# A float32 decoder layer on one core: both feed-forward products by seven block products instead of the second alone

## The chip, the cores and the metric

One core of a Trainium2 chip runs the whole layer in one launch. The metric is the time of an execution on the device in microseconds (us), a median over runs; lower is better. The work is spread over TensorE (PE; its weight loads are listed apart as PEld), VectorE (DVE), ScalarE (ACT), GpSimd (POOL, which here issues DMAs in the feed-forward part) and SyncE (SP, which issues most of the other DMAs).

## The reference

One layer over 512 tokens of width 1024, float32. A mixer comes first (w_in, a gated chunk mixer and a state-space scan, w_out), then the feed-forward part, then a gate with an added per-layer embedding and a last RMSNorm. The change is in the feed-forward part:

```
hid = jax.nn.relu(rmsnorm(h, norm_mlp_g[i]) @ w_ff1[i])   # 512x1024 by 1024x4096
h = h + (hid * hid) @ w_ff2[i]                            # 512x4096 by 4096x1024
```

## The kernel before

**Products.** Every large product is made of three matmuls in the type float32r: each operand is split into a rounded part `hi` and a rest `lo`, and `product` adds hi by hi, lo by hi and hi by lo into one bank of PSUM (lines 1487 to 1489). Each matmul loads 128x128 weights and streams 512 columns. ACT makes `hi` by a copy (`split_form`, line 664), DVE makes `lo` by a subtraction (line 1293).

**Units.** The hidden width of 4096 is worked through in four units of 1024 (`UNITS`). In a unit the first product comes as four *forms* of 512x512 weights of w_ff1 (`product_f1`), each 48 matmuls, an ordinary product. The second product, 512 tokens by 1024 hidden by 1024, is cut in 2x2 blocks and done by Winograd's scheme with seven block products (`product_f2`) of 256 tokens by 512 by 512, 24 matmuls each. Its weight sides are the blocks B11, B21, B22 of w_ff2 and the sums T1 to T4 of blocks; its left sides are blocks A11, A12, A22 of the squared hidden values and sums S1 to S4.

**Forms and buffers.** A form lands in a raw buffer, is split into one of three `ring` buffers, and is then used by PE. The split of form n waits until PE is through with form n-3. There are four raw quarters of 512x512 (`quarter0` to `quarter3`) for w_ff2; the forms of w_ff1 have a raw part in the ring (`ring_raw`). T1 to T4 are summed by DMA: POOL issues a transfer that adds one quarter to another in place (`t_add`, line 568, `quarter<-quarter`), or adds a block from HBM (`quarter<-in_w_ff`). Each form is handled in two pieces, p = 0 and 1, of 512 KB.

**What sets the order.** Each engine runs a list written out by hand, in that order, with semaphores between them: `ff_step` counts PE's steps, `form_hi` and `form_lo` the splits, `q_landed` and `t_landed` the transfers. SP issues loads in a written order too, each after the last reader of its quarter. The results of a second product are added to h by DVE (`h_add`, line 1350) before PE may use the bank again; B11 and T1 are kept in PSUM over all units and added at the end (`h_finish`).

Of the kernel before, what the change touches and what calls it, by code (L numbers as in the profile page):

```python
# [5 lines left out]
P = 128  # L6
F32 = mybir.dt.float32
# [11 lines left out]
TILES = (2, 3, 0, 1)  # L19
UNITS = 4  # L20
STEPS = 30
# [4 lines left out]
SUMS = ("T3", "T2", "T1", "T4")  # L26


def build_layer(nc, a, out):
# [26 lines left out]
    with ExitStack() as ctx:  # L56
# [17 lines left out]
        def form(name, tiles, width):  # L74

            hi = sb(name + "_hi", [P, tiles, width], F32R)
            with ExitStack() as first:
                raw = sb(name + "_raw", [P, tiles, width], where=first)
            lo = sb(name + "_lo", [P, tiles, width], F32R)
            return hi, raw, lo  # L80

        quarter = [sb(f"quarter{i}", [P, 4, 512]) for i in range(2)]
        ring = {0: form("ring0", 4, 512)}
        ring[2] = form("ring2", 4, 512)
        ring[1] = form("ring1", 4, 512)
        quarter += [sb(f"quarter{i}", [P, 4, 512]) for i in range(2, 4)]
        a2 = form("a2", 4, 512)
        s_form = {n: form(f"s{n}", 4, 256) for n in (3, 4, 1, 2)}
        a1 = sb("a1", [P, 4, 512])
        tmp = sb("tmp", [P, 4, 512])  # L90
        with ExitStack() as early:
            conv = sb("conv", [P, 2, 512], where=early)
            xs_t = sb("xs_t", [P, 2, 512], where=early)
# [3 lines left out]
        a11_hi = sb("a11_hi", [P, 4, 256], F32R)  # L97
        a11_lo = sb("a11_lo", [P, 4, 256], F32R)
# [17 lines left out]
        b_hi = sb("b_hi", [P, KT, SEQ], F32R)  # L116
        b_lo = sb("b_lo", [P, KT, SEQ], F32R)
# [77 lines left out]
        f1_landed = [[sem(f"f1_landed{i}{p}") for p in range(2)] for i in range(3)]  # L195
        q_landed = [[sem(f"q_landed{i}{p}") for p in range(2)] for i in range(4)]
        ff_step = sem("ff_step")
        form_hi, form_lo = sem("form_hi"), sem("form_lo")
        gate_hi, gate_lo = sem("gate_hi"), sem("gate_lo")
        t_landed = [[sem(f"t_landed{i}{p}") for p in range(2)] for i in range(2)]  # L200
# [72 lines left out]
        plan += [(("xt", 2, j, q), (2 * j + q + 2) % 4) for j in range(NS) for q in range(2)]  # L273
# [25 lines left out]
        def form_end(n):  # L299

            u, j = divmod(n, FORMS)
            return STEPS * u + (4 * j + 4 if j < 4 else 16 + 2 * (j - 4) + 2)

        def f1_use(n):

            return sum(m % 3 == n % 3 and m % FORMS < 4 for m in range(n + 1))

        def product_end(u, name):

            return STEPS * u + 16 + 2 * PRODUCTS.index(name) + 2  # L310

        def form_count(u, name, p):

            return 2 * (FORMS * u + 4 + PRODUCTS.index(name)) + p + 1

        def hid_bank(u, i):

            return (i + (2 if u else 0)) % 4

        def sum_landed(eng, u, name, p):  # L320

            eng.wait_ge(t_landed[QUARTER[name]][p], 16 * (2 * u + (1 if name in ("T3", "T2") else 2)))

        ADDS = ("T3 right", "T3 above", "T2", "T4", "B21", "B22")
        LAST_ADDS = ("B11 above", "B11 right", "T1 right", "T1 left", "C21", "C12")
# [5 lines left out]
        LO_COUNT = {"A11": 1, "S3": 2, "S2": 3, "S1": 4, "A22": 6, "A12": 6, "S4": 7}  # L331
# [5 lines left out]
        def _(sp):  # L337
# [71 lines left out]
            def load_f1(n):  # L409

                u, e = divmod(n, FORMS)
                b, kh = 2 * u + e // 2, e % 2
                if n >= 3:
                    sp.wait_ge(ff_step, form_end(n - 3))
                else:
                    sp.wait_ge(acc_full, 4 * (OUT + 4) if n < 2 else 4 * (PLE + 1))
                for p in range(2):
                    k = 4 * kh + 2 * p
                    sp.dma_start(ring[n % 3][1][:, 2 * p:2 * p + 2, :], w_ff1[:, k:k + 2, 512 * b:512 * b + 512]
                                 ).then_inc(f1_landed[n % 3][p], 16)  # L420

            def load_quarter(u, name):

                i = QUARTER[name]
                if u:
                    last = {0: "T1", 1: "T4", 2: "B21", 3: "B22"}[i]
                    sp.wait_ge(form_lo, form_count(u - 1, last, 1))
                elif i < 2:
                    sp.wait_ge(lo_ready, 4 * (PLE + 1))
                else:  # L430
                    sp.wait_ge(acc_full, 4 * (PLE + 1))
                row, col = int(name[1]) - 1, int(name[2]) - 1
                for p in range(2):
                    k = 8 * u + 4 * row + 2 * p
                    sp.dma_start(quarter[i][:, 2 * p:2 * p + 2, :], w_ff2[:, k:k + 2, 512 * col:512 * col + 512]
                                 ).then_inc(q_landed[i][p], 16)

            def reload_b12(u):

                for p in range(2):  # L440
                    sum_landed(sp, u, "T2", p)
                    sp.wait_ge(form_lo, form_count(u, "T3", p))
# [3 lines left out]

            load_f1(0)
            load_f1(1)
            load_quarter(0, "B12")
            load_quarter(0, "B11")  # L450
            for s in range(NS):
                sp.wait_ge(*emptied(PLE, s))
                sp.dma_start(ple_dram[s], y[:, s, :]).then_inc(ple_stored[s], 16)
            load_f1(2)
            load_quarter(0, "B22")
            load_quarter(0, "B21")
            load_f1(3)
            reload_b12(0)
            for u in range(1, UNITS):
                load_quarter(u, "B12")  # L460
                load_quarter(u, "B11")
                load_quarter(u, "B21")
                load_f1(FORMS * u)
                load_quarter(u, "B22")
                for e in range(1, 4):
                    load_f1(FORMS * u + e)
                reload_b12(u)

            last = UNITS - 1
            sp.wait_ge(s_raw, 7 * UNITS)  # L470
            sp.wait_ge(hid_lo, 7 * last + LO_COUNT["A11"])
            load_gain(a["final_norm_g"], 0)
            for p in range(4):
                sp.wait_ge(form_lo, form_count(last, "T1" if p < 2 else "T4", 1))
                sp.dma_start(w_raw[:, p], w_gate[:, 2 * p:2 * p + 2, 0:512]).then_inc(w_landed[p], 16)
            sp.wait_ge(ff_step, product_end(last, "T1"))
# [15 lines left out]
        def _(pool):  # L492
# [56 lines left out]
            def t_add(u, name, p):  # L549

                at = (slice(None), slice(2 * p, 2 * p + 2))
                k = 8 * u + 2 * p
                if name == "T3":
                    pool.wait_ge(q_landed[0][p], 16 * (2 * u + 1))
                    pool.wait_ge(q_landed[3][p], 16 * (u + 1))
                    src = quarter[3][at]
                elif name == "T2":
                    sum_landed(pool, u, "T3", p)
                    pool.wait_ge(form_lo, form_count(u, "B11", p))
                    src = quarter[0][at]  # L560
                elif name == "T1":
                    pool.wait_ge(q_landed[0][p], 16 * (2 * u + 2))
# [1250 lines left out]
```

## Time and profile before

| | before |
|---|---|
| median of 3 runs | 748.6 us (747.29 to 748.61) |
| the profiled execution | 747.09 us |
| its span in the trace | 745.3 us |
| PE busy | 735.0 us, 99% |
| DVE, ACT, POOL busy | 61%, 51%, 14% |
| TensorE clock granted | 0.997 of full, mean |

The profiled execution's time is 1.8 us more than its span; that difference lies around the trace. Busy time of PE counts a matmul until its modelled end, and these overlap: a matmul that reads 0.39 us long starts 0.23 us after the one before it, so start-to-start distances are the price of one, not the durations.

### The profile page before, as it was taken

To read this page: it belongs to the slowest core of one execution; us is meant where nothing else is said; L and a number is where in the kernel's file an instruction comes from. 1 tells how busy PE (TensorE), PEld (TensorE's weight loads), DVE (VectorE), ACT (ScalarE), POOL (GpSimd) and SP (SyncE) were. 2 spreads that over 40 slices of the span, in tenths; PEclk is the share of its full clock that TensorE was granted. 3 is DMA by queue.
4 is the path that set the end of the run, shared out by engine and by line. 5 is a ranking of instruction groups with operands and counts; after the bars stand their busy time and mean duration, and the time that the engine had idled before them with its cause. 6 is when DMAs were issued, how large, how long until landed. Compare 5 with 4: busy or idle time off the path is not lost.

```text
span 745.3 us, 8676 instructions
## 1 busy us (share of the span) xinstructions
PE 735.0 (99%) x3396; PEld 606.4 (81%) x3396; DVE 454.1 (61%) x500; ACT 382.9 (51%) x516; POOL 107.3 (14%) x88
## 2 busy tenths in 40 slices
PE   8999999999999999999999999999999999999996
PEld 7888877788878888888888888888888888888884
DVE  5556794576667465546444952576454942589764
ACT  6524456644674833304564633572266524575775
POOL 1031000766455000000012000020001000200000
PEclk9999999999999999999999999999999999999998
DMA  9732223342241163100976685477727792585311
GB/s 332 210 86 86 87 85 99 124 143 86 93 162 57 57 214 125 58 29 14 373 234 148 140 297 150 84 143 231 227 63 156 192 275 97 118 192 178 106 57 56
DMA packets 47872, 105.58 MB, mean 142 GB/s; under 512 B 4668, under 2 KB 6360, under 8 KB 47832
## 3 DMA queue, kind: packets, MB, share of 16 engines
q1 hardware_dynamic: 40968, 84.03, 33.7%
q0 software_dynamic: 5632, 16.78, 12.4%
q10 hardware_dynamic: 1232, 4.23, 1.6%
q8 instruction: 27, 0.44, 0.2%
q14 instruction: 13, 0.11, 0.0%
HBM read 88.21 MB, written 4.23 MB: 124 GB/s over the span
## 4 chain that ended last, share of the span: by engine, by line
PE 98%; DMA 1%; ACT 0%; issue 0%; DVE 0%; SPq 0%; DVEq 0%
PE acc L1487 28%; PE acc L1489 28%; PE acc L1488 28%; PE side L1549 3%; PE side L1488 2%; PE side L1489 2%; PE side L1487 2%; PE side L1646 2%; PE side L1613 1%; PE side L1653 1%; PE side L1641 1%; DMA gain<-in_norm_mix_g 1%; PE acc L1570 0%; PE side L1593 0%; PE side L1594 0%; PE side L1633 0%
## 5 line engine op out<-in xcount | busy, mean ns | idle before, releaser
L1487 PE MATMUL acc<-w_hi,a_hi 128*128 128x512 f32 x256 | 104.5, 408 | 0.0
L1489 PE MATMUL acc<-w_hi,a_lo 128*128 128x512 f32 x256 | 100.2, 391 | 0.0
L1488 PE MATMUL acc<-w_lo,a_hi 128*128 128x512 f32 x256 | 99.9, 390 | 0.0
L1487 PE MATMUL acc<-b_hi,ring_hi 128*128 128x512 f32 x256 | 99.7, 390 | 0.0
L1489 PE MATMUL acc<-b_hi,ring_lo 128*128 128x512 f32 x256 | 99.7, 389 | 0.0
L1488 PE MATMUL acc<-b_lo,ring_hi 128*128 128x512 f32 x256 | 99.7, 389 | 0.0
L664 ACT ACTIVATE ring_hi<-quarter 128x1024 fp32r<-128x1024 f32 x56 | 56.5, 1051 | 51.3 <-PE acc L1489 34.7
L1293 DVE TENSOR_TENSOR ring_lo<-ring_raw,ring_hi 128x1024 fp32r<-128x1024 f32 x32 | 38.6, 1223 | 67.0 <-ACT ring_hi L664 67.0
L1293 DVE TENSOR_TENSOR ring_lo<-quarter,ring_hi 128x1024 fp32r<-128x1024 f32 x56 | 66.0, 1220 | 17.0 <-ACT ring_hi L664 17.0
L568 POOL DMA_DIRECT2D quarter<-quarter x24 | 20.8, 868 | 351.1 <-DMA quarter<-in_w_ff 223.1
L993 DVE TENSOR_TENSOR w_lo<-w_raw,w_hi 128x1024 fp32r<-128x1024 f32 (+1 forms) x40 | 50.8, 1272 | 27.9 <-ACT w_hi L587 27.4
L664 ACT ACTIVATE ring_hi<-ring_raw 128x1024 fp32r<-128x1024 f32 x32 | 33.8, 1056 | 59.3 <-DMA ring_raw<-in_w_ff 59.3
L1487 PEld LDWEIGHTS acc<-w_hi,a_hi 128*128 128x128 f32 x256 | 48.2, 188 | 11.1 <-issue 1.4
L1488 PEld LDWEIGHTS acc<-w_lo,a_hi 128*128 128x128 f32 x256 | 48.2, 188 | 10.6 <-issue 1.4
L1489 PEld LDWEIGHTS acc<-w_hi,a_lo 128*128 128x128 f32 x256 | 48.1, 188 | 10.4
L1488 PEld LDWEIGHTS acc<-b_lo,ring_hi 128*128 128x128 f32 x256 | 48.1, 188 | 10.0
L1487 PEld LDWEIGHTS acc<-b_hi,ring_hi 128*128 128x128 f32 x256 | 48.1, 188 | 10.0
L1489 PEld LDWEIGHTS acc<-b_hi,ring_lo 128*128 128x128 f32 x256 | 48.1, 188 | 9.9
L1487 PE MATMUL acc<-w_hi,b_hi 128*128 128x512 f32 x128 | 50.5, 395 | 0.0
L1489 PE MATMUL acc<-w_hi,b_lo 128*128 128x512 f32 x128 | 50.0, 391 | 0.0
L1488 PE MATMUL acc<-w_lo,b_hi 128*128 128x512 f32 x128 | 49.9, 390 | 0.0
L587 ACT ACTIVATE w_hi<-w_raw 128x1024 fp32r<-128x1024 f32 (+1 forms) x40 | 40.2, 1007 | 15.9 <-PE acc L1489 13.7
(231 smaller groups left out, 1471.8 us busy)
## 6 DMA issues: line engine op xcount, KB each, us to landing
quarter<-in_w_ff SPq DMA_DIRECT2D x40, 512.0 KB, 4.8
w_raw<-in_w_in SPq DMA_DIRECT2D x36, 512.0 KB, 3.7
ring_raw<-in_w_ff SPq DMA_DIRECT2D x32, 512.0 KB, 4.9
quarter<-quarter POOLq DMA_DIRECT2D x24, 512.0 KB, 6.1
w_raw<-in_w_out SPq DMA_DIRECT2D x16, 512.0 KB, 3.4
h<-in_x SPq DMA_DIRECT2D x8, 512.0 KB, 4.3
seg<-cs_dram ACTq DMA_DIRECT2D x8, 512.0 KB, 3.9
quarter<-in_w_ff POOLq DMA_DIRECT2D x8, 512.0 KB, 6.3
```

The costliest lines, as they stand in the source:

```text
L568: pool.dma_start(quarter[QUARTER[name]][at], src, accum_op=ALU.add).then_inc(t_landed[QUARTER[name]][p], 16)
L587: act.activation(w_hi[:, half, 2 * p:2 * p + n, :], w_raw[:, p, 0:n, :], ACT.Copy, scale=scale).then_inc(hi_ready, 1)
L664: act.activation(hi[at], src, ACT.Copy).then_inc(form_hi, 1)
L993: ins = dve.tensor_tensor(lo, raw, hi, ALU.subtract)
L1293: dve.tensor_tensor(lo[at], src, hi[at].bitcast(F32), ALU.subtract).then_inc(form_lo, 1)
L1487: pe.matmul(dst, st[0], mv[0], start=start, stop=False)
L1488: pe.matmul(dst, st[0], mv[1], start=False, stop=False)
L1489: return pe.matmul(dst, st[1], mv[0], start=False, stop=stop)
L1549: ins = pe.transpose(bank[:, i * P:i * P + P], src(i), ident[:])
L1613: filled(pe.matmul(bank.rearrange("p (c n) -> p c n", c=NS), wsT[:, g, :], h[:, :, g * P:g * P + P], start=True, stop=True), ("mix", g))
L1641: filled(pe.matmul(bank, bcT[:, 2 + g, at], carry[:], start=True, stop=True), ("off", j))
L1646: ins = pe.matmul(bank[:, r * HD:r * HD + HD], lm[:, r, :], xdt[:, r * HD:r * HD + HD], start=True, stop=True)
```

## The change

The first product is now done by the seven products too. In each unit the weight sides are blocks of w_ff1 and their sums, in the order `FIRST`, and the left sides (x, shared by all units) are A11, A12, S4, S2, S3, S1, A22 of the normed h, made once ahead of the first unit. A block product of the first product has 256 tokens as its moving side and writes four groups of 256 columns in a pair of banks. DVE then combines the seven results into the four blocks of hidden values (`combine`), after ACT copied two of them out of PSUM (`copy_product`). All weights now go through the four quarters, 14 forms in a unit. T4 is summed in the third buffer, from T2; T1 of the first product is made by DVE (`make_t1`). B22 of the second product now comes fifth. SP's loads stand in the order in which the buffers are released.

```diff
-FORMS = 11
-PRODUCTS = ("B11", "T3", "T2", "T1", "T4", "B21", "B22")
-A_FORMS = ("A11", "S3", "S2", "S1", "A22", "A12", "S4")
-QUARTER = {"T3": 0, "T1": 0, "B12": 0, "B11": 1, "T2": 1, "T4": 1, "B21": 2, "B22": 3}
+FORMS = 14
+FIRST = ("B11", "B21", "B22", "T2", "T3", "T1", "T4")
+FIRST_A = ("A11", "A12", "S4", "S2", "S3", "S1", "A22")
+SECOND = ("B11", "B21", "T3", "T2", "B22", "T1", "T4")
+SECOND_A = ("A11", "A12", "S3", "S2", "S4", "S1", "A22")
+QUARTER = {"T3": 0, "B12": 0, "B11": 1, "T2": 1, "B21": 2, "T4": 2, "B22": 3}
...
+            def load_quarter(u, m, name):
...
+                    if m:
+                        last_use = {"B12": "T3", "B11": "T2", "B22": "T1", "B21": "T4"}[name]
+                        sp.wait_ge(form_lo, form_count(u, 0, last_use, p))
...
+            for u in range(UNITS):
+                load_quarter(u, 1, "B12")
+                load_quarter(u, 1, "B11")
+                load_quarter(u, 1, "B22")
+                load_quarter(u, 1, "B21")
+                reload_b12(u)
+                if u < UNITS - 1:
+                    load_quarter(u + 1, 0, "B11")
+                    load_quarter(u + 1, 0, "B22")
+                    load_quarter(u + 1, 0, "B12")
+                    load_quarter(u + 1, 0, "B21")
...
+            def combine(u, what):
+
+                dst, left, right, op = {
+                    "C11": ("A11", "A21", pair(1), ALU.add), "U": ("A21", pair(1), "A21", ALU.subtract),
+                    "C12 part": ("A12", "A12", "A21", ALU.add), "U3": ("A21", "A21", pair(0), ALU.add),
+                    "C12": ("A12", "A12", pair(1), ALU.add), "C22": ("A22", "A21", pair(1), ALU.add),
+                    "C21": ("A21", pair(0), "A21", ALU.subtract)}[what]
...
+            def product_f1(u, j):
...
+                if j < 2:
+                    pe.wait_ge(*((h_added, add_count(u - 1, ("B22", "T4")[j])) if u else emptied(PLE, 2 + j)))
+                elif j in (2, 4):
+                    pe.wait_ge(p_copied, 2 * u + j // 2)
+                else:
+                    pe.wait_ge(combined, combined_count(u, {3: "C11", 5: "U", 6: "U3"}[j]))
...
+                        ins = product(pair(j % 2)[:, i, :], [t[:, k, i * P:i * P + P] for t in (hi, lo)],
+                                      [t[name][:, k, :] for t in (x_hi, x_lo)], k == 0, k == 3)
```

PE's list at the start of the feed-forward part, before:

```order
L1487 MATMUL acc<-b_hi,ring0_hi 128x512
L1488 MATMUL acc<-b_lo,ring0_hi 128x512
L1489 MATMUL acc<-b_hi,ring0_lo 128x512
L1487 MATMUL acc<-b_hi,ring0_hi 128x512
L1488 MATMUL acc<-b_lo,ring0_hi 128x512
```

And of the change at the same place:

```order
L1641 MATMUL acc<-xA11_hi,ring0_hi 128x256
L1642 MATMUL acc<-xA11_lo,ring0_hi 128x256
L1643 MATMUL acc<-xA11_hi,ring0_lo 128x256
L1641 MATMUL acc<-xA11_hi,ring0_hi 128x256
L1642 MATMUL acc<-xA11_lo,ring0_hi 128x256
```

The 192 matmuls of 512 columns of a unit's first product have become 336 of 256 columns; the second product keeps 168 of 512.

DVE's list in the third unit around the second product, before (`s` and `a2` are left sides):

```order
L1332 TENSOR_TENSOR a2_lo<-a2_raw,a2_hi 128x1024 x2
L1293 TENSOR_TENSOR ring2_lo<-quarter0,ring2_hi 128x1024 x2
L1350 TENSOR_TENSOR h<-h,acc 128x2x512 x2
L1332 TENSOR_TENSOR s4_lo<-s4_raw,s4_hi 128x1024
L1293 TENSOR_TENSOR ring0_lo<-quarter1,ring0_hi 128x1024 x2
L1350 TENSOR_TENSOR h<-h,acc 128x2x512
```

And of the change, in the second unit, from the last `combine` (line 1455; `fS4_raw` is also A21's buffer) to the left side S2:

```order
L1455 TENSOR_TENSOR fS4_raw<-acc,fS4_raw 128x1024
L1476 TENSOR_TENSOR fA12_lo<-fA12_raw,fA12_S1_hi 128x1024
L1429 TENSOR_TENSOR ring2_lo<-quarter0,ring2_hi 128x1024 x2
L1469 TENSOR_TENSOR fS3_raw<-fS4_raw,fA11_S4_raw 128x1024
L1469 TENSOR_TENSOR fS1_raw<-fS4_raw,fA22_raw 128x1024
L1476 TENSOR_TENSOR fS3_lo<-fS3_raw,fS3_hi 128x1024
L1429 TENSOR_TENSOR ring0_lo<-quarter1,ring0_hi 128x1024 x2
L1469 TENSOR_TENSOR fS2_raw<-fA11_S4_raw,fS1_raw 128x1024
L1469 TENSOR_TENSOR fS4_raw<-fA12_raw,fS2_raw 128x1024
L1493 TENSOR_TENSOR h<-h,acc 128x2x512
L1476 TENSOR_TENSOR fS2_lo<-fS2_raw,fA11_S2_hi 128x1024
```

The blocks of hidden values are combined, squared by ACT, subtracted and split while PE is in the first three products of the second product; before, all of A's first half was ready ahead of it.

POOL's list of adding transfers, before, two units:

```order
L568 DMA quarter0<-quarter3 128x1024 x2
L568 DMA quarter1<-quarter0 128x1024 x2
L568 DMA quarter0<-in_w_ff2 128x2x512 x2
L568 DMA quarter1<-quarter2 128x1024 x2
L568 DMA quarter0<-quarter3 128x1024 x2
L568 DMA quarter1<-quarter0 128x1024 x2
L568 DMA quarter0<-in_w_ff2 128x2x512 x2
L568 DMA quarter1<-quarter2 128x1024 x2
```

And of the change, one unit:

```order
L647 DMA quarter0<-quarter3 128x1024 x2
L647 DMA quarter1<-quarter0 128x1024 x2
L647 DMA quarter2<-quarter1 128x1024 x2
L647 DMA quarter0<-quarter3 128x1024 x2
L647 DMA quarter1<-quarter0 128x1024 x2
L647 DMA quarter2<-quarter1 128x1024 x2
L647 DMA quarter0<-in_w_ff2 128x2x512 x2
```

Eight adding transfers in a unit have become 14, and each of T3, T2 and T4 is now made from the one before it.

## Rows read from the trace of the kernel before

**Rows 1.** The page: span, busy time, granted clock in 40 slices.

```profile
span 745.3 us, 8676 instructions
PE 735.0 (99%) x3396; PEld 606.4 (81%) x3396; DVE 454.1 (61%) x500; ACT 382.9 (51%) x516; POOL 107.3 (14%) x88
PEclk9999999999999999999999999999999999999998
```

**Rows 2.** The page's chain that ended last, by engine.

```profile
PE 98%; DMA 1%; ACT 0%; issue 0%; DVE 0%; SPq 0%; DVEq 0%
```

**Rows 3.** Windows: the four units and the rest behind them.

```profile
core 0: us, PE busy (x) PEld busy (x) DVE busy (x) ACT busy (x) POOL busy (x), PEclk, DMA share, GB/s
363.80:445.40 81.60, 81.60 (x362) 67.62 (x361) 47.14 (x43) 38.44 (x47) 9.43 (x10) 1.00 0.77 226
527.00:608.60 81.60, 81.60 (x362) 67.61 (x361) 45.90 (x42) 38.36 (x45) 7.96 (x9) 1.00 0.64 169
690.20:745.30 55.10, 47.95 (x224) 39.62 (x222) 34.23 (x57) 36.72 (x68) 0.00 (x0) 0.96 0.19 69
```

**Rows 4.** Timeline of PE, two matmuls 24 apart: start, duration.

```profile
454.19 0.39 PE L1487 MATMUL acc<-b_hi,ring_hi 128*128 128x512 f32 x1
...
459.63 0.39 PE L1487 MATMUL acc<-b_hi,ring_hi 128*128 128x512 f32 x1
```

**Rows 5.** Timeline: a weight load between two matmuls.

```profile
402.28 0.39 PE L1489 MATMUL acc<-b_hi,ring_lo 128*128 128x512 f32 x1
402.28 0.19 PEld L1487 LDWEIGHTS acc<-b_hi,ring_hi 128*128 128x128 f32 x1
402.51 0.39 PE L1487 MATMUL acc<-b_hi,ring_hi 128*128 128x512 f32 x1
```

**Rows 6.** Chain in order of time: float32 matmuls of 512 and of 64 columns.

```profile
132.71 1.72 PE side L1613 x4
...
146.46 1.73 PE side L1646 x16
```

**Rows 7.** Groups by line in 330 to 700 us: splits and additions.

```profile
L1293 DVE TENSOR_TENSOR ring_lo<-quarter,ring_hi 128x1024 fp32r<-128x1024 f32 x56 | 66.0, 1220 | 17.0 <-ACT ring_hi L664 17.0
L1350 DVE TENSOR_TENSOR h<-h,acc 128x1024 f32<-128x1024 f32 x23 | 28.0, 1219 | 24.8 <-PE acc L1489 24.3
L664 ACT ACTIVATE ring_hi<-quarter 128x1024 fp32r<-128x1024 f32 x56 | 56.5, 1051 | 51.3 <-PE acc L1489 34.7 <-PE side L1489 13.7 <-DMA quarter<-quarter 2.8
```

**Rows 8.** Timeline: two splits back to back on DVE, and on ACT.

```profile
495.52 2.35 DVE L1332 TENSOR_TENSOR s_lo<-s_raw,s_hi 128x1024 fp32r<-128x1024 f32 x2
...
572.51 1.99 ACT L664 ACTIVATE ring_hi<-quarter 128x1024 fp32r<-128x1024 f32 x2
```

**Rows 9.** The page's DMA queues: packets, MB, share of 16 engines.

```profile
q1 hardware_dynamic: 40968, 84.03, 33.7%
q0 software_dynamic: 5632, 16.78, 12.4%
```

**Rows 10.** Landing times of SP's loads of quarters (line 435), of POOL's adding transfers (line 568).

```profile
DMA to landing us min/median/max: 3.8/4.9/11.6
...
DMA to landing us min/median/max: 4.5/6.2/9.7
```

**Rows 11.** Waits in 330 to 745 us: total, times, longest.

```profile
DVE ring_lo L1293 <- ACT ring_hi L664: 84.0, 27, 6.7
```

**Rows 12.** DVE in the last unit, and PE's first transposes for the gate.

```profile
680.17 2.55 DVE L1365 TENSOR_TENSOR h<-h 128x1024 f32<-128x1024 f32 x2
...
688.27 0.87 PE side L1549 x8
```

More of the change, by code:

```diff
@@ L72, in build_layer @@
             gain = sb("gain", [P, 2, D], where=early)
[L74 to L91, printed above, removed]
+            tmp = sb("tmp", [P, 4, 512], where=early)
             conv = sb("conv", [P, 2, 512], where=early)
             xs_t = sb("xs_t", [P, 2, 512], where=early)
+        def split_pair(name, tiles, width):
+            return sb(name + "_hi", [P, tiles, width], F32R), sb(name + "_lo", [P, tiles, width], F32R)
@@ new lines, in raw_lo, with raw_hi @@
+        def raw_lo(name):
+            with ExitStack() as first:
+                raw = sb(name + "_raw", [P, 4, 256], where=first)
+            return raw, sb(name + "_lo", [P, 4, 256], F32R)
+        def raw_hi(name):
+            with ExitStack() as first:
+                raw = sb(name + "_raw", [P, 4, 256], where=first)
+            return raw, sb(name + "_hi", [P, 4, 256], F32R)
+        quarter = [sb(f"quarter{i}", [P, 4, 512]) for i in range(2)]
+        ring = {0: split_pair("ring0", 4, 512)}
@@ new lines, in build_layer @@
+        ring[2] = split_pair("ring2", 4, 512)
+        ring[1] = split_pair("ring1", 4, 512)
+        quarter += [sb(f"quarter{i}", [P, 4, 512]) for i in range(2, 4)]
+        with ExitStack() as early:
+            g_hi = sb("g_hi", [P, KT, SEQ], F32R, where=early)
+            g_lo = sb("g_lo", [P, KT, SEQ], F32R, where=early)
+        x_hi, x_lo, x_raw = {}, {}, {}
+        for name in ("A11", "A12"):
+            x_hi[name], x_lo[name] = split_pair("x" + name, 4, 256)
+        x_raw["A11"], x_hi["S2"] = raw_hi("xA11_S2")
@@ L94, in build_layer @@
+        f_raw["S2"], f_lo["S2"] = raw_lo("fS2")
+        f_lo["A12"] = sb("fA12_lo", [P, 4, 256], F32R)
+        f_raw["S3"], f_lo["S3"] = raw_lo("fS3")
+        f_raw["S1"], f_lo["S1"] = raw_lo("fS1")
         with ExitStack() as early:
@@ L297, in freed, with form_of @@
             ins.then_inc(side_free[fills[name][0]], 1)
-        def form_end(n):
+        def form_of(n):
             u, j = divmod(n, FORMS)
[L302 to L325, printed above, removed]
+            return u, j // 7, (FIRST + SECOND)[j]
+        def form_index(u, m, name):
+            return FORMS * u + 7 * m + (FIRST, SECOND)[m].index(name)
@@ L327, in add_count, with pair @@
+        def pair(i):
+            return acc[:, 2 * i:2 * i + 2, :].rearrange("p a (b n) -> p (a b) n", b=2)
+        ADDS = ("B21", "T3 right", "T3 above", "T2", "B22", "T4")
+        LAST_ADDS = ("B11 above", "B11 right", "T1 right", "C12", "T1 left", "C21")
         def add_count(u, what):
             return 2 + len(ADDS) * u + ADDS.index(what) + 1
-        LO_COUNT = {"A11": 1, "S3": 2, "S2": 3, "S1": 4, "A22": 6, "A12": 6, "S4": 7}
+        COMBINED = ("C11", "U", "C12 part", "U3", "C12", "C22", "C21")
@@ L687, in split_a @@
[L687 to L698 removed]
+                i = home(m, name)
@@ new lines, in _ @@
+                both(5)
+                both(6)
+                both(7)
+                both(8)
+                hidden(u, "A12")
+                split_a(u, "A12")
+                hidden(u, "A22")
+                both(9)
+                hidden(u, "A21")
+                split_a(u, "S3")
+                both(10)
+                split_a(u, "S2")
+                split_a(u, "S4")
+                both(11)
+                both(12)
+                split_a(u, "S1")
+                both(13)
```

699 lines of the change are left out of this document (381 added, 318 removed).

## The prediction

> **What bounds the kernel now.** I read the page first: PE is busy for 735.0 of 745.3 us at the full granted clock [rows 1], and the chain that ended last is 98% PE [rows 2]. Only what shortens PE's list or makes it wait can matter. The windows cut the feed-forward part into four units of 81.6 us, PE busy in all of each, with DVE busy for 45.9, ACT for 38.4 and the DMA engines for 0.64 of it [rows 3]. The timeline gives PE's price: 24 matmuls of 512 columns start over 459.63 - 454.19 = 5.44 us, so 226.7 ns each [rows 4]. A unit has 192 + 168 = 360 of them, and 360 x 226.7 ns = 81.6 us: the whole window, so PE waits for nothing in it. Four units are 326.4 us.
>
> **PE's list.** The first product's 768 matmuls of 512 columns (174.1 us) become 1344 of 256 columns, 12.5% fewer columns. The trace has no float32r matmul of 256 columns, so its price is bounded. From below: half of 226.7 is 113.3 ns, if all of the price goes with the columns. There is a floor near that: float32 records of 512 columns cost 1.72 / 4 = 430 ns each, but those of 64 columns 1.73 / 16 = 108 ns, twice what an eighth of 430 would be [rows 6]. Each has its own load of 128x128 weights, so I read 108 ns as the price of a load, and 256 columns stay above it. From above: a load reads 188 ns long and begins as the matmul before it starts [rows 5]; if the next load could only start when the current matmul does, a matmul would cost 226.7 however short. The 108 ns of [rows 6] speak against that, since loads must overlap each other there. Between the ends I take 120 ns: 512 ticks of the 2.4 GHz level are 213.3 ns, 13.4 are left, and I keep them as a fixed part, 106.7 + 13.4. Then 1344 x 0.120 = 161.3 us, 12.8 less than 174.1. At 113.3 ns it is 152.3, 21.8 less. Break-even is 174.1 / 1344 = 129.5 ns.
>
> The Trainium skill (TensorE: Matmul & The Clock Gate, "Back-to-back issue gap") has N / 2.4 + 2.5 ns for an isolated gap. By that 512 columns would cost 216 ns and 256 would cost 109, and the first product would come out at 146.7 us, 27 less. The 226.7 of [rows 4] for 512 is more than that page has, so I don't take its short fixed part.
>
> **DVE and ACT.** Back to back, an operation of 128x1024 costs 2.35 - 1.22 = 1.13 us on DVE and 1.99 - 1.05 = 0.94 us on ACT [rows 7, 8]; additions that read PSUM last the same 1.22 us [rows 7]. DVE's list for a unit is now 28 splits of forms, 7 combines, 2 for T1, 7 splits and 4 differences of left sides and 6 additions to h: 54 operations, 61 us, where a unit will be 336 x 0.120 + 168 x 0.2267 = 78.4 us. ACT has 28 + 2 copies + 8 for ReLU and square + 7 = 45, 42 us. So neither is the bound on average; before they were at 45.9 and 38.4 of 81.6 [rows 3].
>
> They can be late in one place. Let product 5 of a unit (T1, counted from 0) end at 0. A block product lasts 48 x 0.120 = 5.76 us in the first product and 5.44 in the second, so product 6 ends at 5.8, product 9 starts at 16.6 and product 10, which needs S2, at 22.1. ACT's list from 0 on: form 8 (1.9), ReLU, square and split of A12 (4.9), the same without split for A22 (6.9), form 9 (8.8), ReLU and square of A21, whose last part comes after product 6 (10.8). Then DVE's difference S3 (12.1), ACT's split of it (13.1) and of form 10 (15.1), DVE's rest of form 10 (16.3), the differences S2 and S4 (18.8), B21's addition to h (19.9), and the rest of S2 at 21.1. That is 1.0 us ahead of product 10. The start is less sure than that: form 8 is B21 of w_ff2, loaded into the third quarter only after form 6 (T4) was split, and form 6's split waits for product 3, which ended at -11.5, and on DVE for two combines behind it. It is through at -7.7 and -6.6; with 4.9 us to landing [rows 10] the pieces are there at -2.8 and -1.7. But the two adding transfers of T3 stand in the same DMA engines then. By [rows 9] a piece of 0.524 MB holds all 16 engines for 0.337 x 745.3 / 84.03 x 0.524 = 1.6 us as a load and 0.124 x 745.3 / 16.78 x 0.524 = 2.9 us as an addition. Two of these in between make the second piece land at about 3, where ACT wants it at 1. So the chain comes out up to 1 us late for product 10, and 3 us where both additions and a load collide. I take 1.2 us of waiting for each unit, 4.8 in all, between 0 and 12.
>
> In the first unit the x side is added: 4 differences and 5 splits on DVE and their copies on ACT, in front of or between the splits of forms 1 to 5. It starts as soon as the last tile is transposed, with two forms ahead, and costs 9 x 1.13 = 10 us on DVE out of the 17 us of slack (78.4 - 61). I take 1.5 us, between 0 and 5. Behind the last product, the first transposes of the gate [rows 12] need T1's addition and C12's, which before were over 5 us earlier: 680.17 + 2.55 = 682.7 against 688.27. Now both come after product T1, 2 x 1.2 = 2.4 us against half of T4's 5.44, 2.7. I take 0.2, at most 2. Copies out of PSUM and combines sit one product (5.8 us) ahead of the bank's next use with two or three operations before them; at nothing, and 1.1 us for each operation that is late.
>
> **DMA.** A unit has 18 loads and 14 adding transfers: 18 x 1.6 + 14 x 2.9 = 69 us of the DMA engines in 78.4 us, 88%, where before it was 18 x 1.6 + 8 x 2.9 = 52 in 81.6, 0.64, as the window shows [rows 3]. It fits, with little left. The chain T3, T2, T4, each after the other, has two rounds in a unit. A round is a load (4.9), three additions (3 x 6.2, [rows 10]) and a split (2.3): 26 us of half a unit's 39. POOL only issues.
>
> **Sum.** -12.8 + 4.8 + 1.5 + 0.2 = -6.3. Against the profiled execution's 747.1 that is 740.8. The median of the runs shown is 1.5 above it, and I predict that: 742.3 us.
>
> **Rivals.**
> *Cheaper still.* The price goes with the columns (113 ns) and waiting is small: -21.8 + 6 = -16, 733 us. For it: that nothing in the trace says the 13.4 ns are fixed. Against: the shorter PE's part, the earlier it asks for DVE's, so that waits grow where PE's list shrinks.
> *Waiting eats it all, slower.* The place above: if the chain to S2 and the one to S4 behind it (form 11, two additions to h and a split, 5.7 us against a product of 5.44) are late together by over 3.2 us in each unit, the 12.8 are gone. With 5 us for each unit the sum is -12.8 + 20 + 1.7 = +9, 757 us. For it: DVE has 13 operations in a row there with no gap; DVE now waits 84.0 us for ACT's halves over the part [rows 11], and every such wait inside this stretch goes to PE. Against: only the late piece of form 8 starts it.
> *The DMA engines become the bound.* If packets take a quarter longer than now, 69 becomes 86 us for each unit, 4.6 more than 81.6: +18, 765 us. It decides from 18% on. For it: adding transfers already took up to 9.7 us [rows 10]. Against: in the first unit 0.77 was held without a wait [rows 3].
> *Loads don't overlap short matmuls.* A matmul of 256 columns then costs 108 + 107 = 215 ns, 289 us for the 1344, +115, 862 us. Against it: by the same rule 512 columns would cost 108 + 213 = 321, and [rows 4] has 226.7. The Trainium skill (TensorE: Matmul & The Clock Gate, "What overlaps and what doesn't") has loads overlap running matmuls only when the row group differs, which here it never does; the trace disagrees, since in [rows 5] the load runs inside the matmul.
> *No change.* The waits make up 11 to 14 us: within 0.2%.
>
> **Numbers.** The forecast (1.5 to 13 us faster) has 0.58, cheaper still 0.10, no change 0.10, waiting 0.12, DMA 0.07, loads 0.03. About 0.2% (1.5 us) is what a measurement of this kernel can tell from no change. So faster 0.68, the same 0.10, slower 0.22. The range leaves out the loads, the DMA rival and half of the waiting above, and the far end of the cheap case below: 732 to 753 us.
>
> **What the profile after would show.** The first product's matmuls 120 ns apart (right), 113 or over 130 (wrong). DVE busy for about 61 us and ACT for 42 in a unit, DMA share near 0.88. PE idle, if anywhere, ahead of the second product's third to fifth block products, released by DVE's `lo` of S2 or S4, 1 to 1.5 us a unit. T3's and T2's additions landing in under 9 us. It would be wrong if PE waits over 3 us a unit, if transfers of T2 or of the reloaded B12 end ACT's waits in every round, or if the price is over 129 ns.

## The result and the profile after

| | before | after |
|---|---|---|
| median of 4 runs | 747.94 us (747.23 to 748.61) | 754.92 us (752.95 to 756.94) |
| the profiled execution | 747.09 us | 752.95 us |
| its span | 745.3 us | 751.2 us |

The ratio is 1.0094, 95% interval 1.0062 to 1.0125: the change makes the kernel 7 us slower, where 742.3 us (732 to 753) had been forecast. The profiled execution is its fastest, 2.0 us under its median, and shows 5.9 of them.

The page after, in the parts that answer to [rows 1, 2, 9, 10] (span, busy time; queues with their share of 16 engines; the chain that ended last, by engine and by line; landing times):

```profile
span 751.2 us, 10013 instructions
PE 729.8 (97%) x3972; PEld 625.7 (83%) x3972; DVE 529.2 (70%) x553; ACT 415.7 (55%) x525; POOL 128.0 (17%) x112
...
q1 hardware_dynamic: 40968, 84.03, 33.7%
q0 software_dynamic: 9088, 29.36, 21.2%
...
PE 71%; DVE 10%; DMA 9%; ACT 7%; issue 3%; SPq 0%; ACTq 0%; DVEq 0%
PE acc L1641 20%; PE acc L1643 20%; PE acc L1642 20%; DMA quarter<-in_w_ff 8%; DVE ring_lo L1429 4%; PE side L1706 3%; ACT ring_hi L769 2%; PE side L1803 2%; DVE h L1493 1%; ACT fA_raw L781 1%; DVE fS_lo L1476 1%; ACT fA_S_hi L802 1%; PE side L1770 1%; PE side L1641 1%; DVE fS_raw L1469 1%
...
quarter<-in_w_ff SPq DMA_DIRECT2D x72, 512.0 KB, 6.7
quarter<-quarter POOLq DMA_DIRECT2D x48, 512.0 KB, 6.1
```

The chain, 98% PE before, is 71% PE now. DMA, DVE and ACT stand in it with 26%: the path that ends last goes through loads of w_ff blocks and the splits and sums made from them. q0, the queue of the adding transfers, carries 29.36 MB where it carried 16.78. A load of a quarter now lands after 6.7 us in the median, where it took 4.8 to 4.9 before; an addition as before after 6.1.

Windows of the same kernel, cut at the switches between first and second product, then the gate (they answer to [rows 3]):

```profile
core 0: us, PE busy (x) PEld busy (x) DVE busy (x) ACT busy (x) POOL busy (x), PEclk, DMA share, GB/s
365.90:406.20 40.30, 40.30 (x338) 40.30 (x337) 37.10 (x33) 24.60 (x25) 4.77 (x7) 1.00 0.84 214
406.20:450.50 44.30, 40.66 (x171) 32.48 (x170) 36.54 (x32) 27.06 (x27) 7.96 (x9) 0.96 0.94 224
450.50:490.80 40.30, 40.30 (x338) 40.30 (x337) 27.97 (x24) 22.03 (x23) 5.84 (x7) 1.00 0.74 185
490.80:530.20 39.40, 39.01 (x171) 31.30 (x170) 33.62 (x29) 21.76 (x22) 7.08 (x9) 1.00 0.99 240
530.20:570.50 40.30, 40.30 (x338) 40.30 (x337) 29.09 (x25) 23.23 (x24) 5.79 (x7) 1.00 0.73 184
570.50:609.80 39.30, 38.68 (x170) 31.31 (x169) 33.62 (x29) 21.40 (x22) 6.99 (x8) 1.00 0.98 240
609.80:650.10 40.30, 40.30 (x337) 40.27 (x336) 29.09 (x25) 22.18 (x23) 5.57 (x7) 1.00 0.75 184
650.10:692.40 42.30, 39.91 (x179) 32.20 (x178) 39.78 (x38) 25.29 (x30) 4.34 (x5) 1.00 0.80 222
692.40:743.30 50.90, 48.05 (x217) 39.48 (x215) 31.75 (x51) 35.31 (x65) 0.00 (x0) 0.97 0.13 48
```

Read the lengths first. All four first products take 40.3 us, which is 336 x 0.120: not one wait, and 12.8 us less for the four than the 174.1 of the kernel before. The second products should take 168 x 0.2267 = 38.1 us each. They take 44.3, 39.4, 39.3 and 42.3 (0.9 of the last are the gate's first transposes): 6.2 + 1.3 + 1.2 + 3.3 = 12.0 us too long. The gate behind them takes 50.9 us, where before it took 46.2 (691.7 to 737.9): 4.7 more. The feed-forward part begins 1.5 us later, at 365.9 instead of 364.4 (PE's first matmul of w_in starts at 12.6 instead of 10.8, and 0.3 of that is made up on the way), and the end behind the gate is 0.5 longer. In all -12.8 + 12.0 + 4.7 + 1.5 + 0.5 = +5.9, which is the difference of the two spans.

The list of PE's waits after, from 365 us on (total, times, longest):

```profile
PE acc L1641 <- DVE fS_lo L1476: 3.4, 2, 2.6
PE acc L1641 <- DVE w_lo L1107: 2.9, 1, 2.9
PE side L1706 <- DVE h L1506: 1.4, 1, 1.4
PE acc L1641 <- DVE fA_lo L1476: 1.1, 1, 1.1
PE side L1641 <- DVE fS_lo L1476: 0.6, 2, 0.5
```

`fS_lo` and `fA_lo` are left sides of the second product, `w_lo` is the gate's weights, `h` is C12's last addition ahead of the transposes. These are 9.4 us. In the first unit PE waits at product 8 for A12 (1.1) and at product 9 for S3 (2.6); products are counted from 0 in a unit, 7 to 13 being the second product's. The rest of the 16.7 lies in shorter delays and in this (timeline of PE after, around the wait of 2.6 us, then around the one of 2.9):

```profile
418.25 0.39 PE L1643 MATMUL acc<-ring_hi,fA_lo 128*128 128x512 f32 x1
421.20 0.58 PE L1641 MATMUL acc<-ring_hi,fS_hi 128*128 128x512 f32 x1 [2.57 <-DVE fS_lo L1476]
421.58 0.63 PE L1642 MATMUL acc<-ring_lo,fS_hi 128*128 128x512 f32 x1
422.01 0.63 PE L1643 MATMUL acc<-ring_hi,fS_lo 128*128 128x512 f32 x1
...
710.76 0.50 PE L1641 MATMUL acc<-w_hi,g_hi 128*128 128x512 f32 x1 [2.85 <-DVE w_lo L1107]
...
712.39 0.63 PE L1643 MATMUL acc<-w_hi,g_lo 128*128 128x512 f32 x1
712.82 0.63 PE L1641 MATMUL acc<-w_hi,g_hi 128*128 128x512 f32 x1
```

Behind both waits the matmuls start 0.43 us apart instead of 0.227. The windows of those two stretches show it as granted clock:

```profile
711.50:714.90 3.40, 3.40 (x10) 2.63 (x9) 2.52 (x4) 1.65 (x6) 0.00 (x0) 0.52 0.02 5
421.40:424.80 3.40, 3.40 (x9) 2.64 (x9) 3.37 (x4) 0.60 (x2) 2.42 (x2) 0.51 0.48 110
```

So in each of the two windows PE runs at 1.2 instead of 2.4 GHz, which costs about 1.7 of their 3.4 us.

**What is behind the wait of the first unit.** The timelines of SP, POOL, ACT and DVE after, for B21 of w_ff2 (form 8, third quarter):

```profile
387.12 4.06 ACT L769 ACTIVATE ring_hi<-quarter 128x1024 fp32r<-128x1024 f32 x4
390.47 1.22 DVE L1171 TENSOR_TENSOR xA_lo<-xA_raw,xA_hi 128x1024 fp32r<-128x1024 f32 x1
391.61 1.22 DVE L1476 TENSOR_TENSOR fA_lo<-fA_S_raw,fA_S_hi 128x1024 fp32r<-128x1024 f32 x1
392.74 1.22 DVE L1455 TENSOR_TENSOR fS_raw<-acc,fS_raw 128x1024 f32<-128x1024 f32 x1
394.06 1.23 DVE L1455 TENSOR_TENSOR fA_raw<-fA_raw,fS_raw 128x1024 f32<-128x1024 f32 x1
395.21 2.35 DVE L1429 TENSOR_TENSOR ring_lo<-quarter,ring_hi 128x1024 fp32r<-128x1024 f32 x2
396.45 1.50 SPq L517 DMA_DIRECT2D quarter<-in_w_ff  x2
397.25 0.85 POOL L647 DMA_DIRECT2D quarter<-quarter  x1 [19.85 <-DMA quarter<-in_w_ff]
398.52 0.85 POOL L647 DMA_DIRECT2D quarter<-quarter  x1 [0.42 <-issue]
407.37 1.06 ACT L769 ACTIVATE ring_hi<-quarter 128x1024 fp32r<-128x1024 f32 x1 [4.65 <-DMA quarter<-in_w_ff]
```

ACT has made its half of T4 (form 6) by 391.2. Four operations of DVE stand ahead of DVE's half: x's A22, A11's split and the combines U and C12 part. So that half starts at 395.21; the two loads of B21 follow it, and the two additions of T3 are issued between and behind them. The second piece, issued at 397.6, lands 9.8 us later, at 407.4. ACT has been waiting 4.65 us for it. Everything behind on ACT and DVE (A12, A22, S3) is late by that: product 8 waits for A12, and product 9, which needs S3, waits 2.6 us behind 418.25.

### The profile page after: what moved, and what is told of

The parts are those of the page before. It is cut to its first block, busy times and chain, and to the rows that moved or that the text cites. A ratio compares the mean times of both kernels' runs of the same rounds, so it can differ in the third digit from the quotient of the medians.

```text
span 751.2 us, 10013 instructions
## 1 busy us (share of the span) xinstructions
PE 729.8 (97%) x3972; PEld 625.7 (83%) x3972; DVE 529.2 (70%) x553; ACT 415.7 (55%) x525; POOL 128.0 (17%) x112
## 3 DMA queue, kind: packets, MB, share of 16 engines
q1 hardware_dynamic: 40968, 84.03, 33.7%
q0 software_dynamic: 9088, 29.36, 21.2%
## 4 chain that ended last, share of the span: by engine, by line
PE 71%; DVE 10%; DMA 9%; ACT 7%; issue 3%; SPq 0%; ACTq 0%; DVEq 0%
PE acc L1641 20%; PE acc L1643 20%; PE acc L1642 20%; DMA quarter<-in_w_ff 8%; DVE ring_lo L1429 4%; PE side L1706 3%; ACT ring_hi L769 2%; PE side L1803 2%; DVE h L1493 1%; ACT fA_raw L781 1%; DVE fS_lo L1476 1%; ACT fA_S_hi L802 1%; PE side L1770 1%; PE side L1641 1%; DVE fS_raw L1469 1%
## 5 line engine op out<-in xcount | busy, mean ns | idle before, releaser
L769 ACT ACTIVATE ring_hi<-quarter 128x1024 fp32r<-128x1024 f32 x112 | 113.3, 1050 | 94.3 <-PE acc L1643 47.2
L1429 DVE TENSOR_TENSOR ring_lo<-quarter,ring_hi 128x1024 fp32r<-128x1024 f32 x112 | 132.8, 1221 | 41.4 <-ACT ring_hi L769 41.3
L647 POOL DMA_DIRECT2D quarter<-quarter x48 | 41.4, 862 | 341.8 <-DMA quarter<-in_w_ff 249.8
L1642 PE MATMUL acc<-xS_lo,ring_hi 128*128 128x256 f32 x256 | 72.4, 283 | 0.0
L1100 DVE TENSOR_TENSOR w_lo<-w_raw,w_hi 128x1024 fp32r<-128x1024 f32 x36 | 48.1, 1337 | 27.7 <-ACT w_hi L668 27.3
L1641 PEld LDWEIGHTS acc<-w_hi,a_hi 128*128 128x128 f32 x256 | 48.1, 188 | 10.8 <-issue 1.4
L1643 PEld LDWEIGHTS acc<-w_hi,a_lo 128*128 128x128 f32 x256 | 48.0, 188 | 10.4
L1643 PE MATMUL acc<-xA_hi,ring_lo 128*128 128x256 f32 x192 | 54.3, 283 | 0.0
L1641 PE MATMUL acc<-xS_hi,ring_hi 128*128 128x256 f32 x192 | 54.3, 283 | 0.0
L1643 PE MATMUL acc<-xS_hi,ring_lo 128*128 128x256 f32 x192 | 54.3, 283 | 0.0
L1642 PE MATMUL acc<-xA_lo,ring_hi 128*128 128x256 f32 x192 | 54.3, 283 | 0.0
L1641 PE MATMUL acc<-xA_hi,ring_hi 128*128 128x256 f32 x192 | 54.3, 283 | 0.0
L1642 PEld LDWEIGHTS acc<-xS_lo,ring_hi 128*128 128x128 f32 x256 | 49.2, 192 | 0.0
L1641 PE MATMUL acc<-a_hi,w_hi 128*128 128x512 f32 x96 | 38.9, 405 | 0.0
L1643 PE MATMUL acc<-ring_hi,fS_lo 128*128 128x512 f32 x96 | 38.1, 396 | 0.0
```

Of the source, the lines that this page charges most:

```text
L647: pool.dma_start(quarter[home(m, name)][at], src, accum_op=ALU.add).then_inc(t_landed[home(m, name)][p], 16)
L769: act.activation(ring[n % 3][0][at], quarter[i][at], ACT.Copy).then_inc(form_hi, 1)
L1100: ins = dve.tensor_tensor(lo, raw, hi, ALU.subtract)
L1429: dve.tensor_tensor(lo[at], src, hi[at].bitcast(F32), ALU.subtract).then_inc(form_lo, 1)
L1641: pe.matmul(dst, st[0], mv[0], start=start, stop=False)
L1642: pe.matmul(dst, st[0], mv[1], start=False, stop=False)
```

## The experiments

Ratios are to the kernel before, with the 95% interval.

**The change again, unaltered, and three edits of one order each.**

> The changed kernel unaltered, to compare the others with on one chip. Theory 1 (waits at few fixed places eat the 12.8 us): ratio to before 1.009, the first unit's second product again about 6 us longer than its 38.1, the later ones 1 to 1.5, and PE waiting 3 us in the gate. Theory 2 (the start of the program differs): in the first profile w_in's first matmul came at 12.58 us against 10.82 before; if that belongs to the change it is there again, if it is scatter it comes out elsewhere between 10.5 and 13.

Measured: 754.58 us, 1.0093 (1.0068 to 1.0117), runs from 751.2 to 759.1, where the kernel before stays within 747.1 and 748.6. In this execution product 8 of the first unit waited 1.5 us, product 9 2.95 - 0.23 = 2.7 us, product 10 another 1.3, and the later units 0.6 to 1.4 each at product 10. The four second products take 44.5, 39.3, 40.0 and 42.9 us, the first without a stretch at half clock, and the gate 50.7. What the waits of the second product cost differs from run to run; that it costs about as much as the shorter list gives does not. PE's first matmul of w_in starts at 10.8 here as in the kernel before, so the 1.5 us at the start belong to the execution and not to the change.

> Only the order of eight instructions each on ACT and DVE: the pieces 2 and 3 of the second half of the gate's weights are split ahead of the first sigmoid, not behind it. Theory 1: PE's wait of 2.9 us in the third group of the gate goes, and with it the stretch at half the granted clock behind it (1.7 us): 3 to 5 us faster than the changed kernel, ratio to before about 1.003. Rival (the gate is late because T4's addition to h comes last and the sigmoids with it): PE waits later instead, at the fifth group, for the first sigmoid, and the time stays within 1 us.

```diff
-                if i < 2:
-                    for p in (2 * i, 2 * i + 1):
+                if i == 0:
+                    for p in range(4):
                         split_gate(1, p)
```

Measured: 750.67 us, 1.0036 (1.0014 to 1.0057). PE's wait for `w_lo` is gone from its list, and the gate takes as long as before (window of its gate, clock at 1.00):

```profile
695.50:741.60 46.10, 46.10 (x217) 38.34 (x215) 31.78 (x51) 35.08 (x65) 0.00 (x0) 1.00 0.14 52
```

So this place was worth 0.57%, 4.2 us, where the gate had grown by 4.7: 2.9 of waiting and 1.7 of half clock behind it. In this execution product 9 waits in three units, for 2.7, 1.9 and 2.4 us counted in the same way, where in the profile after it did in one: that is the scatter.

> Only DVE's order inside a unit: form 6's rest (T4 of the first product) is made ahead of C12's part, of A11's rest and, in the first unit, of the x side's A22. Theory 1 (B21 of w_ff2 lands late because its quarter is released late by DVE): the first unit's second product falls from 44.3 to 40 to 42 us, the later ones from 39.4 to 38.1 to 38.8; 3 to 5 us faster than the changed kernel. Rival (the landing is late because the DMA engines are shared with T3's additions): B21's second piece still takes 7 us or more and the units shrink by under 1 us each, 0 to 2 us in all.

```diff
                 both(5)
-                if u == 0:
-                    x_split("A22")
-                split_a(u, "A11")
                 combine(u, "U")
+                both(6)
                 combine(u, "C12 part")
-                both(6)
+                if u == 0:
+                    x_split("A22")
+                split_a(u, "A11")
                 combine(u, "U3")
```

Measured: 746.69 us, 0.9985 (0.9972 to 0.9997), runs from 745.5 to 747.3. The edit moves C12 part, x's A22 and A11's split behind T4's; U stays ahead of it. This one edit of DVE's order is worth 1.1%, 8 us, and the scatter is gone with it (1.8 us over four executions, where the change run again had 7.9 over six). B21's second piece is issued at 392.7 instead of 397.6 and lands at 398.9 instead of 407.4. Of these 4.9 us, 1.3 are the earlier start of the whole part in this execution; the other 3.6 are about what the three operations take (3 x 1.13 = 3.4). It also lands in 6.2 us instead of 9.8: both loads are now issued ahead of T3's additions (395.6 and 396.8). The windows of its four second products:

```profile
404.90:446.00 41.10, 39.20 (x170) 31.26 (x169) 35.04 (x31) 23.02 (x24) 6.81 (x8) 1.00 0.95 228
486.30:525.20 38.90, 38.71 (x170) 31.36 (x169) 33.52 (x29) 21.43 (x22) 6.91 (x8) 1.00 0.98 234
565.60:604.10 38.50, 38.42 (x170) 31.36 (x170) 33.61 (x29) 22.22 (x23) 6.72 (x7) 1.00 0.98 236
644.40:685.30 40.90, 39.34 (x178) 31.99 (x177) 39.53 (x38) 23.87 (x28) 4.18 (x4) 1.00 0.81 221
```

41.1, 38.9, 38.5 and 40.9 us: 5.9 us shorter than in the profile after. The DMA engines are as busy as there (0.95 to 0.98 in the first three, 0.81 in the last), and DVE's work is the same; only where the split of T4 stands differs. No unit waits at product 8 or 9 any more; the gate, whose weights this edit leaves where they were, still takes 50.9.

> In the second product T3's additions by DMA are held until B21 has landed, so that B21's load has the DMA engines alone. Rival (sharing with T3's additions makes B21 late): B21's second piece lands in about 5 us rather than 9.8, ACT's wait of 4.7 us for it goes, and the first unit gets 1 to 3 us shorter unless T3 is late next. Theory 1 (released late, sharing matters little): T3 lands 4 to 5 us later, form 9 waits for it, and the kernel is the same or up to 4 us a unit slower.

```diff
                     pool.wait_ge(q_landed[3][p], quarter_count(u, m, "B22"))
+                    if m:
+                        pool.wait_ge(q_landed[2][p], quarter_count(u, m, "B21"))
```

Measured: 754.44 us, 1.0078 (1.0046 to 1.0111), the same as the change. The load was helped: B21's second piece landed in 4.3 us instead of 9.8. The time was not, since T1, the last of POOL's chain, is now late (waits of PE in this kernel; `side` is product 12's bank):

```profile
PE side L1643 <- DVE fS_lo L1478: 3.9, 3, 2.6
```

So the additions do slow that load, and product 9's wait is gone in all units; but the time is moved to T1, whose second piece ACT waits for until 432.2. The run shifts the collision and does not remove it. That B21's late start is what costs rests on the run before this one, where an earlier start, with the additions left as they are, gave the time back.

**The price of columns by itself, two orders more, and all four together.**

> Nothing of the layer: PE alone runs 72 float32r matmuls each, every one with its own weight load, of 512 (twice), 384, 320, 256, 192, 128 and 64 columns, and the input is stored as the output. Theory of the prediction (columns at 2.4 GHz and 13.4 ns fixed): 227, 173, 147, 120 ns, and from 192 columns down a floor at 108 to 112 where the weight load sets the price. Rival (price goes with columns until the floor): 227, 170, 142, 113. A second rival: below 256 columns float32r gets dearer than the floor.

The kernel issues 72 float32r matmuls for each width with a new weight load ahead of each:

```diff
+            for n in (512, 512, 384, 320, 256, 192, 128, 64):
+                for i in range(72):
+                    ins = pe.matmul(acc[:, i % 2, 0:n], st[:, i % 4, :], mv[:, 0:n], start=True, stop=True)
```

Measured in one execution, windows that begin and end with a width's 72 matmuls (512, 384, 320, 256, 192 and 128 columns), and one stretch within the last width (64 columns):

```profile
27.47:43.79 16.32, 16.32 (x74) 13.51 (x72) 0.00 (x0) 0.00 (x0) 1.00 0.00 1
43.79:56.30 12.51, 12.51 (x74) 12.51 (x73) 0.00 (x0) 0.00 (x0) 1.00 0.01 1
56.30:66.85 10.55, 10.55 (x74) 10.55 (x73) 0.00 (x0) 0.00 (x0) 1.00 0.00 0
66.85:75.48 8.63, 8.63 (x74) 8.63 (x73) 0.00 (x0) 0.00 (x0) 1.00 0.01 2
75.48:83.50 8.02, 8.02 (x74) 8.02 (x73) 0.00 (x0) 0.00 (x0) 1.00 0.00 0
83.50:91.51 8.01, 8.01 (x74) 8.01 (x73) 0.00 (x0) 0.00 (x0) 1.00 0.01 2
...
97.00:99.00 2.00, 2.00 (x11) 2.00 (x11) 0.00 (x0) 0.00 (x0) 0.50 0.00 0
```

Divided by 72: 226.7, 173.8, 146.5, 119.9, 111.4 and 111.3 ns. From 512 to 256 columns each is its columns at 2.4 GHz plus 13.2 to 13.8 ns; 192 columns would be 93.4 by that rule and cost 111.4, as 128 do. So there is a fixed part of about 13.4 ns and a floor of 111 ns, and 256 columns lie just above the floor. 64 columns have no price at full clock here: the granted clock fell to 0.50 within them, with PE busy all the while.

> In the first unit DVE's two sums of quarters of h (2.3 us) are made 14 us earlier, where DVE waited 1.6 us for ACT, and no longer between U3 and form 7. If DVE's list before the second product sets the first unit's waits: 1 to 3 us faster than the changed kernel. If the late landing of B21 sets them: within 1 us, since form 8 is late all the same.

```diff
                 if u == 0:
                     x_split("S1")
+                    dve.wait_ge(xn_ready, 2 * NS)
+                    dve.tensor_tensor(h21, h21, h22, ALU.add).then_inc(h_added, 1)
+                    dve.tensor_tensor(h12, h12, h22, ALU.subtract).then_inc(h_added, 1)
                 both(5)
```

(and the same three lines taken out ahead of `both(7)`). Measured: 755.09 us, 1.0091 (1.0071 to 1.0111): no difference. The two sums leave the stretch behind T4's split and stand ahead of it instead, and neither place is better. That fits the late landing of B21 as what sets the first unit's waits.

> The order of gate_weights_first, and T1's addition and C12 ahead of the gate's first weights on DVE. Theory: PE's wait of 1.4 us for C12 in the middle of the last product goes as well, another 1 to 2 us on top of what gate_weights_first gives, 4 to 6 us faster than the changed kernel. Rival: the gate's first weights are late instead and PE waits at the gate's first group by as much.

To the edit of the gate's weights it adds one on DVE:

```diff
-            split_gate(0, 0)
             h_finish("T1 right")
             h_finish("C12")
+            split_gate(0, 0)
             split_gate(0, 1)
```

Measured: 748.81 us, 1.0016 (0.9999 to 1.0033), 0.2% below the gate's weights alone, which the two intervals do not tell apart; PE's list shows it, where the wait for C12 went from 1.4 to 0.2 us.

> T4's split first, the sums of h early, and both orders of the tail together, nothing else changed. If the waits are those places and they add up: 12.8 less 1 to 3 us of waits are left, ratio to before 0.985 to 0.992. If another resource stands behind them (the DMA engines at 0.98 in the second products): waits reappear in the second product and the ratio stays above 0.996.

Measured: 740.88 us (738.6 to 743.2), 0.9908 (0.9891 to 0.9925). The four orders add up within the intervals: 1.0093 - 0.0108 (T4's split) - 0.0057 (gate's weights) - 0.0020 (C12) - 0.0002 (h sums) = 0.9906. What PE still waits for from 365 us on (the longest of five):

```profile
PE side L1640 <- DVE fS_lo L1476: 1.8, 2, 1.5
...
```

It keeps all 14 block products and every transfer and addition of the change, at the same DMA shares (0.99, 0.98, 0.98 and 0.83 in the second products). This is the version to take: 0.9% faster than the kernel before and 1.8% faster than the change.

**What is left in it: T1's chain, and A22's part of the T4 edit.**

> all_orders, and T1 of the second product made by DVE from T2 and B22 as in the first product (two operations, ahead of the T3 additions to h), so that the reload of B12 and T1's additions from HBM go: 2 loads and 2 adding transfers fewer for each unit, 9 us of DMA engine time. Theory (the 5 us of waits left in all_orders hang on the DMA chain that ends in T1): product 12's waits (0.4 to 1.7 us) go, 2 to 4 us faster than all_orders. Rival (DVE is the tighter one there, 33.6 us busy of 39): product 11 waits for S4 by 1 to 2 us in each unit, 2 to 6 us slower than all_orders.

```diff
+                for p in range(2):
+                    make_t1(u, p, 1)
                 h_add(u, "T3 right")
                 h_add(u, "T3 above")
```

with T1's reload of B12 and its additions on POOL taken out, and the next unit's B12 loaded first of its quarters. Measured: 751.13 us, 1.0048 (1.0036 to 1.0061). The DMA share in the second unit's second product fell from 0.98 to 0.71, and PE's waits went up (waits from 365 us on, and the window of that product):

```profile
PE acc L1629 <- DVE fS_lo L1463: 9.6, 4, 2.4
...
488.60:529.40 40.80, 38.42 (x171) 31.40 (x170) 35.79 (x31) 21.60 (x23) 4.30 (x5) 1.00 0.71 177
```

Each unit waits 2.4 us at product 11 for S4: two operations of DVE, 2.3 us, stand in its chain where DVE has no room.

> As t1_by_dve_early, with T1 made behind the rest of S4 in DVE's list. Theory: the same gain without the wait at product 11; T1's split is then later by 3.5 us and product 12 has still 1 to 2 us in hand: 736 to 739 us. Rival: product 12 waits 1 to 2 us a unit, no faster than all_orders.

The same with `make_t1` behind the split of S4. Measured: 744.67 us, 0.9959 (0.9948 to 0.9971); now product 12 waits, 1.2 us in each of four units:

```profile
PE side L1629 <- DVE fS_lo L1463: 4.6, 4, 1.2
```

Both are slower than T1 by the DMA engines (0.9908), though these are at 0.98 there. In this stretch DVE's order is dearer than the DMA engines' share.

> The changed kernel with one move of t4_split_first alone: in the first unit the x side's A22 is split behind form 6 on DVE (1.1 us earlier for form 6, there only). If the first unit's 6 us come from the x side's extra operations: its second product falls by 1.5 us or more, the later units stay. If they come from the order in every unit (U, C12's part and A11 ahead of form 6): 0 to 1.5 us in all, and t4_split_first's gain is that of the order.

Only `x_split("A22")` goes behind `both(6)`. Measured: 750.22 us (747.6 to 755.0), 1.0034 (1.0013 to 1.0055). B21's second piece is issued at 395.1, and the first unit's second product takes 41.2 us instead of 44.3, but the later ones still 39.9, 41.1 and 41.4. About half of the gain of the T4 edit (0.59 of 1.08%, each to some 0.3%) is this one operation in the one unit; the other half goes with the other two operations (C12 part and A11's split), and only the whole edit takes the scatter away (here it is 7.4 us over twelve executions).

> all_orders without T1's two additions from HBM in the second product: the reloaded B12 stands in for T1, a wrong weight side, the same work on PE, ACT and DVE. It takes out 5.8 us of DMA engine time a unit and the end of the chain, and adds nothing to DVE. Theory (T1's late landing sets product 12's wait): the waits at product 12 go, those at products 10 and 11 (0.3 us each) stay; 1.5 to 4 us faster than all_orders. Rival: as slow as all_orders within 1 us, then DVE's list holds product 12.

This kernel leaves out T1's two additions, so its second product is not the layer's. Measured: 738.94 us, 0.9883 (0.9869 to 0.9898), 0.25% (1.9 us) below all orders, with intervals that just overlap. The waits of product 12 are gone; the first line left is product 10's in the first unit (1.2, where all orders had 0.3):

```profile
PE acc L1642 <- DVE fS_lo L1478: 1.2, 1, 1.2
...
```

So T1's additions set product 12's waits in the version with all orders, and they are worth about 1.9 us.

## Why the prediction was wrong

**PE's price: right.** I took 120 ns between 113.3 and 226.7. The first products are 336 x 0.120, and the widths by themselves show the fixed 13.4 ns that I had read out of 226.7. The gain of this term, 12.8 us, is there within a tenth. "Loads don't overlap short matmuls" is out, and "cheaper still" too: 113 ns would be the columns without the fixed part, and the floor lies at 111. Here the Trainium skill (TensorE: Matmul & The Clock Gate, "Back-to-back issue gap") has N / 2.4 + 2.5 ns for an isolated gap, by which 256 columns would be an estimated 109; the run has 119.9, and the measurement decides.

**The busy times and DMA: right.** DVE has 28.0 + 33.6 = 61.6 us in the second unit (61 predicted), ACT 43.8 (42), and the DMA share is the mean of 0.74 and 0.99, 0.86 (0.88). An added MB takes what [rows 9] gave: 0.212 x 751.2 / 29.36 = 5.4 us of all engines, 5.5 there. So "the DMA engines become the bound" didn't happen: packets took no longer, and with all orders the same shares go with 740.9 us. What I had not read out of a mean of 0.88 is that it is made of 0.74 and 0.99, with loads that land after 6.7 us and not after my 4.9, and additions that took up to 10.4 where I had under 9.

**The step that failed: the waiting.** "I take 1.2 us of waiting for each unit, 4.8 in all, between 0 and 12", "In the first unit ... I take 1.5 us" and "I take 0.2" for the turn to the gate. Measured were 6.2 in the first unit and 1.3, 1.2 and 3.3 in the others, the turn's 1.4 included: 12.0 where I had 6.5. The mechanism was the one named, B21 landing late behind T4's split with T3's additions in its way; what failed is when that split is through in the first unit. I had it wait "for product 3 ... and on DVE for two combines behind it" and be through "at -7.7 and -6.6", counted from the end of product 5, and the second piece of B21 land "at about 3". Product 5 ends at 400.4: the piece was issued at -2.8 and landed at 6.9. The two combines are U and C12 part. I had left out x's A22 and A11's split, which stand ahead of them in DVE's list: I put the x side's operations to the 17 us of DVE's slack, and an order has no slack. With T4's split ahead of A22, A11 and C12 part the piece is issued at -6.5 and lands at -0.3, and 1.1% of the time comes back. In the later units of the change it is issued at -5.5 to -5.9 and lands at -0.4 to 2.3, inside what I had, and these units wait little.

The sum also compared the chain with product 10 alone. In the first unit PE stopped earlier, at products 8 and 9. The second and third unit have my 1.2 us, but in part by luck: the waits are spread over products 10 to 12, the longest (0.5) at product 12, which my sum did not look at. The turn to the gate, at 0.2 in the sum, waited 1.4.

**The place that I had not named: the gate, +4.7.** In the sum it stood at nothing. T4 is the last product, and its addition to h comes ahead of the last of the norm's sums. So ACT's splits of the second half of the gate's weights begin 9.2 us into the gate (701.6), where before they began 5.7 into it; half of them stand behind the first sigmoid, at 708.6, and PE waits 2.9 us for them at 707.9. I followed T1's and C12's additions to the gate's transposes, but not the gate's own weights.

**What a wait costs beyond itself.** The two longest waits, 2.6 and 2.9 us, each had a stretch at half clock behind them, 1.7 us each. Neither the sum nor a rival had that. It makes the one wait of product 9 worth 4.3 us in this execution; behind the same wait in the run again the clock stayed up.

**The rivals.** "Waiting eats it all, slower" is what happened, but not as 5 us in each unit: as 6.2 in one, 3.3 in the last and 4.7 in the gate. "No change" had the right amount of waiting for the feed-forward part: that part is 0.8 us shorter than before. In this execution it is the gate, and the 1.5 at the start, that make it slower. Executions above it would have longer waits of the second product: the profile with the gate's edit has 169.9 us for its four, where the one after has 165.3.

What stays open: why the waits of product 9 fall in different units in different executions of the change. The runs show only that none of the five profiles with T4's split first has one.

## What to carry to other kernels

Where PE's list gets shorter, cost the other engines' lists not by their sum against the window but by position: for each transfer that now starts late, count every operation that stands ahead of the release of its buffer in that engine's list, the first unit's extra ones too, and put the release first. A DMA share is to be read for each half of a stage: here a mean of 0.86 was made of 0.74 and 0.99. When the last product of a stage changes, follow all that its last addition holds up in the next stage, the next stage's own weights included.

## What the runs showed of the hardware

A float32r matmul with a load of 128x128 weights ahead of each costs its columns at 2.4 GHz plus 13.2 to 13.8 ns from 256 to 512 columns, and 111 ns at 192 and 128. In the layer's kernel the loads read 188 to 192 ns each, longer than the 120 ns from one matmul of 256 columns to the next, so by the records two loads are under way at once. The granted clock fell to half behind some of PE's waits of 2.2 us and more (2.2 and 2.6 at product 9, 2.4 at product 11, 2.9 in the gate) and not behind others as long (2.6 in the run again), and behind none of the four waits of 1.2 us with T1 made late by DVE. In the run on columns it fell with PE busy throughout, at 64 columns. Adding transfers took 5.4 us of all 16 engines for each MB, plain loads 0.337 x 751.2 / 84.03 = 3.0.
